# Gate tiles as products of high parts and remainders, split by GpSimd, in a two-layer hybrid decoder step

## What is computed

```python
h = rmsnorm(x, lp['norm1_g'])
z = h @ lp['w_in']                     # branch inputs and, as gate_raw, 4 x 1024 gate columns
a_out = u * gmlp_spatial(v, ...)       # A: spatial gating
b_out = mla_attention(...)             # B: latent attention, prompt and 1024 cached tokens per decode row
o, s_new = gdn_chunked(...)            # C: gated DeltaNet with a short causal convolution on q, k, v
m_out = mem_attention(mq, mem_k, mem_v)  # M: cross attention into 256 memory tokens
gates = sigmoid(gate_raw.reshape(n, t, 4, D_MODEL))
x = x + einsum('ntbd,ntbd->ntd', gates, proj) @ lp['w_out']
x = x + hier_moe(rmsnorm(x, lp['norm2_g']), lp)
```

## Time and profile before

| | us |
|---|---|
| median of 3 runs | 1592.44 |
| lowest, highest | 1591.14, 1599.42 |
| the profiled execution | 1583.4 |
| its span, first to last instruction | 1581.6 |
| TensorE busy (with overlaps taken out) | 1319.4 |
| VectorE, ScalarE, GpSimd busy | 788.6, 336.4, 37.4 |
| gate products, busy on TensorE, both layers | 251.1 |

### The profile page before, as it was taken

How to read it: one execution, slowest core, us unless ns; L and a number is a source line. 1 busy time by engine, 2 the same in 40 slices (tenths; PEclk the granted TensorE clock), 3 DMA queues, 4 the chain that set the end, 5 groups by cost and what they waited for, 6 DMA issues and landing times. The chain is left out here.

```text
span 1581.6 us, 22386 instructions
## 1 busy us (share of the span) xinstructions
PE 1319.4 (83%) x8246; PEld 925.1 (58%) x8246; DVE 788.6 (50%) x1754; ACT 336.4 (21%) x662; POOL 37.4 (2%) x40
## 2 busy tenths in 40 slices
PE   6988968987889789878789889689788897798785
PEld 3967756976567534524349666569665675344242
DVE  4754656466453524333346656564654635343342
ACT  0222504111121212202011225131111213212120
POOL 0040000000000000000000400000000000000000
PEclk9998989988999799999879989899788997999998
DMA  5562012125245589999734610221261546999996
GB/s 187 160 203 63 0 45 81 51 83 224 70 145 205 213 335 372 384 409 370 312 117 160 213 53 1 55 71 53 80 246 48 177 174 248 361 375 385 409 380 263
DMA packets 89949, 307.63 MB, mean 195 GB/s; under 512 B 16369, under 2 KB 19201, under 8 KB 88193
## 3 DMA queue, kind: packets, MB, share of 16 engines
q1 hardware_dynamic: 86784, 295.92, 50.8%
q0 software_dynamic: 3072, 10.49, 1.9%
HBM read 403.05 MB, written 3.98 MB: 257 GB/s over the span
## 5 line engine op out<-in xcount | busy, mean ns | idle before, releaser
L564 PE MATMUL bank<-hT,reused 128*128 128x264 f32 x512 | 125.4, 404 | 15.3 <-PEq L271 10.0
L564 PE MATMUL bank<-hT,reused_l 128*128 128x264 f32 x512 | 125.7, 405 | 14.2 <-PEq L271 9.7
L564 PEld LDWEIGHTS bank<-hT,reused 128*128 128x128 f32 x512 | 100.6, 200 | 36.3 <-issue 11.8
L564 PEld LDWEIGHTS bank<-hT,reused_l 128*128 128x128 f32 x512 | 100.9, 200 | 35.5 <-issue 11.5
L2423 DVE TENSOR_TENSOR xT<-xT,bank 128x264 f32<-128x264 f32 x112 | 46.7, 429 | 72.1 <-PE bank L2179 70.0
L2143 PE MATMUL bank<-moe_w,reused 128*32 128x512 f32 x256 | 33.5, 646 | 10.4 <-DMA moe_w<-in_w_x 10.4
L2143 PE MATMUL bank<-moe_w_l,reused_l 128*32 128x512 f32 x256 | 33.9, 651 | 9.2 <-DMA moe_w_l<-in_w_x 9.2
L2178 PE MATMUL bank<-moe_Q,moe_high 128*128 128x264 f32 x96 | 30.9, 343 | 10.7 <-DVE xT L2423 5.4
L337 DVE TENSOR_TENSOR moe_low_l<-bank,moe_high_l 128x512 fp32r<-128x512 f32 x24 | 15.5, 686 | 48.5 <-ACT moe_high_l L2273 48.5
L337 DVE TENSOR_TENSOR moe_low<-bank,moe_high 128x512 fp32r<-128x512 f32 x24 | 15.5, 686 | 47.9 <-ACT moe_high L2273 47.9
L2178 PE MATMUL bank<-moe_Q_l,moe_high_l 128*128 128x264 f32 x96 | 30.0, 336 | 10.8 <-DVE xT L2423 5.4
(11 more groups left out here) (1026 smaller groups left out, 2782.8 us busy)
## 6 DMA issues: line engine op xcount, KB each, us to landing
moe_w<-in_w_x SPq DMA_DIRECT2D x176, 512.0 KB, 10.4
moe_w_l<-in_w_x SPq DMA_DIRECT2D x176, 512.0 KB, 11.0
early<-in_w_x SPq DMA_DIRECT2D x76, 512.0 KB, 10.8
early_l<-in_w_x SPq DMA_DIRECT2D x76, 512.0 KB, 11.4
reused<-in_w_x SPq DMA_DIRECT2D x36, 512.0 KB, 11.7
reused_l<-in_w_x SPq DMA_DIRECT2D x36, 512.0 KB, 11.9
reused<-in_w_gate SPq DMA_DIRECT2D x32, 512.0 KB, 3.6
reused_l<-in_w_gate SPq DMA_DIRECT2D x32, 512.0 KB, 3.6
```

Source lines behind the costliest of these rows:

```text
L564: mm = pe.matmul(E["bank"][to][:, 0:T], F["wf"][slot][:, k, :], E["hT"][:, k, :], start=k == 0, stop=k == KT - 1)
```

## The change

Gate tiles are multiplied as the projection's tiles are: three one-pass products of high parts and remainders. The parts of h (`hsp`), which the projection makes anyway, are kept through the stages to `memory` in place of `hT`; the weight tile is split by GpSimd, with a copy (float32 to fp32r) and a subtraction, into one of two pairs of buffers (`wsp`). The load of a tile waits for the split of the tile that used its `wf` buffer before, and the split waits for the tile's load and for the multiplication of the tile two before it. Each stage's GpSimd program gets the splits of its tiles, and the last splits and loads of a stage prepare the first tiles of the next: the projection loads tiles 0 to 3 and splits 0 and 1, `mla_decode` prepares `gdn`, `gdn` prepares `memory`. In `mla_prompt` the splits stand between and behind the gathers, ahead of the reordering copies.

To make room, scratch tiles of several stages are laid into rows of the shared buffer (`zT`, the area behind the weight buffers) that no longer hold live data, and the third early expert tile moves in the same buffer. Engine loops are written out, with the same instructions in each round; in the solve, tiles now use both buffers in turn.

```diff
+def gate_load(sp, S, A, l, F, slot, tile, splits=0):
+
+    if splits:
+        sp.wait_ge(S(f"gw{slot}_split"), splits)
+    sp.dma_start(F["wf"][slot][:], A["w_gate"][l, tile]).then_inc(S(f"gw{slot}_loaded"), 16)
+
+
+def gate_split(nc, pool, S, F, slot, loads, splits, used=0):
+
+    (high, low), whole = F["wsp"][slot], F["wf"][slot]
+    if loads:
+        pool.wait_ge(S(f"gw{slot}_loaded"), 16 * loads)
+    if used:
+        pool.wait_ge(S("gate_done"), used)
+    nc.gpsimd.tensor_copy(high[:], whole[:]).then_inc(S(f"gw{slot}_high"), 1)
+    pool.wait_ge(S(f"gw{slot}_high"), splits)
+    low_part(nc.gpsimd, low[:], whole[:], high[:]).then_inc(S(f"gw{slot}_split"), 1)
...
     for k in range(KT):
-        mm = pe.matmul(E["bank"][to][:, 0:T], F["wf"][slot][:, k, :], E["hT"][:, k, :], start=k == 0,
-                       stop=k == KT - 1)
+        mm = multiply_split(pe, E["bank"][to][:, 0:T], [w[:, k, :] for w in F["wsp"][slot]],
+                            [h[:, k, :] for h in F["hsp"]], start=k == 0, stop=k == KT - 1)
```

In `project`, `memory`, `mla_prompt`, `mla_decode` and `gdn`, in this order:

```diff
             for i in range(2):
                 gate_load(sp, S, A, l, F, i, i)
             for i in range(2):
-                sp.wait_ge(S(f"gw{i}_loaded"), 16)
+                gate_load(sp, S, A, l, F, i, 2 + i, 1)
+            for i in range(2):
+                sp.wait_ge(S(f"gw{i}_loaded"), 32)
             sp.wait_ge(S("v_ready"), 2)
             sp.dma_start(A["o_gv"][l], gv[0:NS_TOK, 2, :]).then_inc(S("v_stored"), 16)
             sp.wait_ge(S("v_stored"), 16)
+
+        @ph.b.gpsimd
+        def _(pool):
+            for i in range(2):
+                gate_split(nc, pool, S, F, i, 1, 1)
+            for i in range(2):
+                pool.wait_ge(S(f"gw{i}_split"), 1)
...
+        @ph.b.gpsimd
+        def _(pool):
+            for r in range(2, 8):
+                gate_split(nc, pool, S, F, r % 2, r // 2 - 1, r // 2, used=r - 1)
...
                 pool.indirect_dma_start(B["kr"][:, n, :], None, A["kr"], rows).then_inc(E["kr_loaded"], 16)
+                if n in (3, 5):
+                    r = n // 2 + 1
+                    gate_split(nc, pool, S, F, r % 2, 0, 1, used=r - 1)
+            for r in range(4, MLA_TILES):
+                gate_split(nc, pool, S, F, r % 2, r // 2 - 1, r // 2, used=r - 1)
             pool.wait_ge(E["kr_loaded"], 16 * NS_TOK * (l + 1))
...
             for i in range(2):
                 gate_load(sp, S, A, l, F, i, MLA_TILES + i)
-            for i in range(2):
-                sp.wait_ge(S(f"gw{i}_loaded"), 16)
+            gate_load(sp, S, A, l, F, 0, MLA_TILES + 2, 1)
+            sp.wait_ge(S("gw0_loaded"), 32)
+            sp.wait_ge(S("gw1_loaded"), 16)
+
+        @ph.b.gpsimd
+        def _(pool):
+            gate_split(nc, pool, S, F, 0, 1, 1)
+            pool.wait_ge(S("gw0_split"), 1)
...
-            for r in range(2, 9):
-                gate_load(sp, S, A, l, F, r % 2, MLA_TILES + r, used=r - 1)
-            with sp.Fori(1, 7) as k:
-                gate_load(sp, S, A, l, F, 1, MLA_TILES + 8 + k, used=k + 8)
-            gate_load(sp, S, A, l, F, 0, MLA_TILES + 15, used=9)
-
+            for r in range(3, GDN_TILES + 2):
+                gate_load(sp, S, A, l, F, r % 2, MLA_TILES + r, (r - 1) // 2)
...
+        @ph.b.gpsimd
+        def _(pool):
+            for r in range(1, GDN_TILES + 2):
+                gate_split(nc, pool, S, F, r % 2, (r - 1) // 2, (r + 1) // 2, used=max(r - 1, 0))
...
-            with pe.Fori(1, 7) as k:
+            for k in range(1, 7):
...
-                gate_multiply(pe, S, E, F, 1, k + 3, 7, k + 8)
+                gate_multiply(pe, S, E, F, k % 2, (k + 9) // 2, 7, k + 8)
```

More of the change, by code:

```diff
@@ L361, in project @@
         wsp = [[ph.sb(f"wsp{i}{part}", [P, KT, P], F32R) for part in range(2)] for i in range(2)]
-        hsp = [ph.sb(f"hsp{part}", [P, KT, T], F32R) for part in range(2)]
+        hT = ph.sb("hT", [P, KT, T])
         uT = ph.sb("uT", [P, 2, T])
@@ L381, in _ @@
                     .then_inc(S("bias_loaded"), 16)
-            with sp.Fori(1, FM_N // 2) as t:
+            for t in range(1, FM_N // 2):
                 for i in range(2):
@@ L445, in _ @@
                  wait=False)
-            with dve.Fori(3, MIX_AT + 1) as t:
+            for t in range(3, MIX_AT + 1):
                 split(t)
@@ L458, in _ @@
             step(tt(brT[:, 0:2, :], mixed[:], uT[:], ALU.mult))
-            with dve.Fori(MIX_AT + 1, FM_N // 2) as t:
+            for t in range(MIX_AT + 1, FM_N // 2):
                 split(t)
@@ L493, in _ @@
                 tile(i)
-            with pe.Fori(1, MIX_AT) as t:
+            for t in range(1, MIX_AT):
                 pair(t)
@@ L508, in _ @@
             mm.then_inc(S("vT_done"), 1)
-            with pe.Fori(MIX_AT, FM_N // 2) as t:
+            for t in range(MIX_AT, FM_N // 2):
                 pair(t)
@@ L537, in _, with gate_multiply @@
                 .then_inc(S("vroot_ready"), 1)
-            with act.Fori(2, FM_N // 2) as t:
+            for t in range(2, FM_N // 2):
                 pair(t)
 MLA_TILES, GDN_TILES = 8, 16
[L548 to L560, removed]
+def gate_load(sp, S, A, l, F, slot, tile, splits=0):
[11 more added lines that the diff above has]
+    low_part(nc.gpsimd, low[:], whole[:], high[:]).then_inc(S(f"gw{slot}_split"), 1)
+def gate_multiply(pe, S, E, F, slot, splits, to, copied=None):
+    if splits:
+        pe.wait_ge(S(f"gw{slot}_split"), splits)
     if copied is not None:
@@ L884, in _ @@
             sp.dma_start(wuk[:], A["w_uk"][l]).then_inc(S("wuk_loaded"), 16)
-            for r in range(2, MLA_TILES):
-                gate_load(sp, S, A, l, F, r % 2, r, used=r - 1)
+            for r in range(4, MLA_TILES):
+                gate_load(sp, S, A, l, F, r % 2, r, r // 2 - 1)
             sp.wait_ge(S("latent_ready"), 2)
@@ L1602, in _ @@
             nc.scalar.activation(e1[:, 1], gb[:, 1], ACT.Exp).then_inc(S("wG_done"), 1)
-            with act.Fori(1, 7) as k:
+            for k in range(1, 7):
                 for j in range(2):
@@ L1699, in _ @@
                      f"x{j}_ready", wait=False)
-            with dve.Fori(1, 7) as k:
+            for k in range(1, 7):
                 for j in range(2):
@@ L1834, in _ @@
             sp.dma_start(wrt[:], A["w_rt"][l]).then_inc(S("wrt_loaded"), 16)
-            with sp.Fori(1, KT // 2) as i:
+            for i in range(1, KT // 2):
                 for s in range(2):
@@ L1863, in _ @@
             pair(0)
-            with pe.Fori(1, KT // 2) as i:
+            for i in range(1, KT // 2):
                 pair(i)
@@ L1903, in _ @@
             sigmoid(1)
-            with act.Fori(2, KT) as dt:
+            for dt in range(2, KT):
                 sigmoid(dt)
@@ L1943, in _ @@
                 .then_inc(S("wrt_ready"), 1)
-            with dve.Fori(1, KT // 2) as i:
+            for i in range(1, KT // 2):
                 pair(i)
@@ L1988, in branches @@
                  for s in range(EARLY - 1)]
-        early.append([reused[:, half * g:half * g + half] for g in range(4)])
-        kept = dict(xTM=xTM, early=early, rest=reused[:, 4 * half:])
+        early.append([reused[:, z + half * g:z + half * g + half] for g in range(4)])
+        kept = dict(xTM=xTM, early=early, rest=reused[:, 0:z])
         mix(nc, A, dict(E, **kept), l, F)
```

136 lines of the change are left out of this document (74 added, 62 removed).

## The result

The changed kernel takes 1635.0 us in the median of four runs (1633.3 to 1639.4); the kernel before, beside it, 1591.8 (1587.7 to 1599.4). The ratio is 1.0297, with a 95% interval of 1.0261 to 1.0333: slower by 43 us. The forecast was 1633 with a range of 1580 to 1660. The profiled execution of the changed kernel took 1639.4 us with a span of 1637.4, so it is 55.8 us longer than the profiled execution of before.

What follows compares the result with a forecast made beforehand. Each stage ends in a barrier, so its latest engine bounds it; gate tiles count only where TensorE is last. Terms of 8 + 4.4 + 12 - 4 = 20.4 us a layer, 40.8 for two, gave 1633 us, range 1580 to 1660.

Steps and rivals of the forecast that it cites:

- The projection, +8: Projection's end: load, split, load and store in series on SyncE outlast TensorE, 8 us a layer, bounds 6 and 10.
- The price of a split: GpSimd copy 1.03 us plus subtraction 2.06: 3.1 us a split, 3.4 with gaps, ends 2.1 and 3.9.
- The hold: GpSimd and VectorE take turns: each split in a run of two-SBUF-input VectorE instructions delays it by 3.1 us.
- The DeltaNet stage, +12: DeltaNet, a layer: SiLU +9.5, decay chain +5.2, split 10 +2, loop -3.9, last tile -0.8; bounds +4 and +19.
- the 2.1 of cover: DeltaNet decay chain: TensorE reached the reader 2.1 us after the chain's result, so a 7.3 us hold adds only 5.2.
- the clock of the first: All stages: lengths were forecast for one layer, in the clock of the first layer.
- The latent prompt, +4.4: Latent attention, prompt: tile 4 late 3.7 us, softmax products 1.8, tile 7 gains 1.1; bounds +1.4 and +7.
- pays split 3, which hides behind tile 4: Latent prompt: VectorE's dense run from 102.5 to 108.1 is held by split 3, at no cost to the stage.
- Memory, -4: Memory attention, a layer: tiles 0 and 1 gain 1.7 us, tile 5 ends at 392.1; sum -4, bounds -5.5 and -2.5.
- no stalls: Rival: GpSimd and VectorE work side by side; -7.7 us a layer, 1577 us, faster; chance 0.18.
- VectorE keeps its turn: Rival: GpSimd can't get between waiting VectorE instructions, convolution ends on time; +2.3 us a layer, 1597 us; chance 0.15.
- the dear subtraction: Rival: GpSimd's subtraction takes 2.9 us or more; 1645 to 1665 us; chance 0.14.

Runs made afterwards that it cites:

- run with idle copies: Kernel before plus unneeded GpSimd work at the DeltaNet stage's start, copy/subtraction pairs in layer 1, sixteen copies in layer 2: 1606.3 us beside 1578.0, ratio 1.0157.
- second profile: The changed kernel itself, unaltered, run and profiled again beside the kernel before on the same chip: ratio 1.0331.

## Why the prediction was right, and where it was not

**The projection, +8: right.** From the last zT copy to the next stage it became 6.9 and 7.8 us longer, by the chain that the prediction names, and shorter by 4.4 and 4.9 when only this chain was cut. The second layer's stage shows +4.5 because TensorE had its last copy done 72.0 us after the start there, not 75.3, at a granted clock of 0.96 instead of 0.91.

**The price of a split: right within its bounds.** The copy takes 1.04 us undisturbed (1.03 forecast), the subtraction 2.34 (2.06 taken, bounds 1.03 and 2.9). Of the two anchors, twice the disturbed copy was too dear and two undisturbed copies too cheap. The Trainium skill, GPSIMD Engine Reference (3.1), had led to an estimate of 2.25: the nearer one, as it turned out.

**The hold: right as a mechanism, and wider than the prediction said.** It spoke of VectorE instructions with two SBUF inputs. The run with idle copies shows that one-input TENSOR_SCALARs are held too, and the decay chain's copies from SBUF to SBUF (6.50 us for 1.43). Not held were RECIPROCAL (6.75 us before and after), TENSOR_REDUCE (1.22) and products that read PSUM (four in 1.27), beside a split and without one. The Trainium skill, SBUF — State Buffer (who interferes with whom), lists copies and TENSOR_SCALAR in their two-port modes beside two-input instructions and leaves reductions out; these runs agree, with the numbers above.

**The DeltaNet stage, +12, came to +18.3: the terms of the sum were near, and two things were left out.** Counted from the stage's start: the convolution ends 14.4 us later (15.3 forecast) and SiLU begins 8.5 later (9.5). The decay chain is held for 4.8 us where 7.3 were forecast, but the 2.1 of cover that the forecast took off is gone, because tile 7 had itself waited 5.3 us for ScalarE's copy of tile 5; so what the chain's reader adds is 6.6, not 5.2. From there to the loop 1.6 are added (2 forecast for split 10). The rounds behind the first gain 0.66 each (0.65).

The first thing left out is TensorE's clock. The square sums and the loop's first products by time, before, then after (the latter's second row stands above, at 313.74), then the loop's first products of the kernel with written-out loops:

```profile
241.72 2.05 PE L1451 MATMUL bank<-gdn_sq,cst 128*128 128x264 f32 x8 [1.04 <-DVE gdn_sq L1640]
...
277.45 2.05 PE L1493 MATMUL bank<-gdn_X,gdn_MT 128*128 128x128 f32 x16 [2.05 <-DVE gdn_MT L1705]
...
267.94 3.89 PE L1482 MATMUL bank<-gdn_sq,cst 128*128 128x264 f32 x8 [7.92 <-DVE gdn_sq L1671]
...
284.57 3.40 PE L1493 MATMUL bank<-gdn_X,gdn_MT 128*128 128x128 f32 x16 [1.38 <-DVE gdn_MT L1705]
```

TensorE now waits 7.9 us for the squares instead of 1.0, and their sums take 3.89 us instead of 2.05, at a granted clock of 0.50; the run with idle copies shows the same behind such a wait. This puts the reciprocal 10.4 us late instead of 8.5. Tile 7, behind its wait of 5.3 us, also ran at 0.50, and the decay sums are 17.0 late. The loop's first products are 18.6 late and take 3.79 us instead of 2.05, at 0.51, which eats more than two rounds' gain. That these last were slow because of the change is not shown: the kernel with written-out loops has no split, and there they took 3.40 in the first layer, and the stage was 3.3 and 3.0 us longer than before. The profile of before was taken in an execution 8.4 us below that kernel's median, so a part of the 18.3 may lie in the execution that was profiled. Over the stretch up to the loop the granted clock is 0.78, and was 0.97. The forecast took "the clock of the first" for granted while it made TensorE wait.

The second is the tail. Before the second round the stage is 19.7 late, before the sixth 17.1, and where the tile behind the loop starts 16.3. That tile gains 0.6, yet the stage ends 18.2 late: splits 16 and 17 cost some 2.5 us there, as the run that moved them shows, in which the products of L1581 are 15.7 late instead of 18.5.

**The latent prompt, +4.4, came to +8.9 and +4.2, and to +14.9 and +4.3 in the second profile.** The step that failed is the sentence that the query run "pays split 3, which hides behind tile 4". It doesn't hide: the transposes of q stand ahead of tile 4 on TensorE, and wait for VectorE's run and ScalarE's copies behind it. In the second profile the four rotary products of that run took 7.41 us instead of 1.54, held by splits 4 and 5, and the transposes end 42.2 us after the stage's start, 9.2 behind split 4. In the first profile one product of the run took 2.77 us instead of 1.01, and the two paths end close together: split 4 is done 33.1 us after the start (32.7 forecast), the transposes 34.6 after it; in the second layer these are 32.5 and 32.8. So in the first layer most of the +8.9 are terms of the sum that came out larger: the lateness behind tile 4 was 5.9 us, not 3.7 (it began 6.4 late, and ran in part at half clock), the softmax products lost 2.4, not 1.8, and tile 7 gained 0.2, not 1.1. With whole tiles the stage is back at 59.7.

**Memory, -4: right**, -4.1 and -4.3. **Decode, mix, experts, loops and scratch, 0: right**, with +0.8 and +0.5 for decode.

**The sum.** The terms gave 40.8 us between the profiles; it was 55.8, and the missing 15 are mostly the DeltaNet stage (12.7) and the first layer's latent stage (4.5), less the second projection (3.5). The forecast added 9 us for the kernel's median above its profiled run; the profiled run of the changed kernel was itself 4.4 above its median. So part of the closeness of 1633 and 1635 is two errors that meet. Between the medians it was 43 us. Of the rivals, "no stalls" falls with the idle splits, "VectorE keeps its turn" with the convolution's rows, and the dear subtraction with 2.34 us.

## What to carry to other kernels

A helper engine whose instructions take turns with those of the busy one is not free work: price each of its instructions as a hold on every instruction of the other that it can meet, and ask where the hold goes when it is moved, since delaying it only chooses another victim. Give it the stretches in which the other engine waits for PSUM or runs reciprocals (here the solve loop and the memory stage, 0.7% faster), and leave the rest as it was. When a change makes TensorE wait for long, ask what the products behind the wait cost at half clock (here 1.8 us for the square sums, behind 7.9 us of waiting).

## What was unexpected in the hardware

- Cutting a GpSimd instruction in four lets more VectorE instructions through, but costs about 0.17 us for each instruction: a copy of 128x256 takes at least 0.39 us, of 128x1024 1.04; a subtraction 0.71 and 2.34.
- Sixteen GpSimd copies (17.3 us busy) hold the convolution for 12.6 us, nearly as much as five copies and five subtractions (17.2 us) do with 14.7: what counts is in the main GpSimd's time, and less which instruction it is.
- The same program had its latent prompt stage of the first layer at 68.6 and at 74.6 us, where a split began 2.8 us after the rotary products did, when they were already through, or 0.2 us after, when they were not.
